# Eight picks of the first search gathered first, head 3's query between the first groups, and another order of slots

## The chip, the cores and the metric

The kernel runs on one core of a Trainium2 chip, in one launch. The metric is the device time of that launch in microseconds (us). Measured before the change: 1631.8 us as the median of 3 runs, from 1630.57 to 1632.56.

The engines are TensorE (PE, matmuls; PEld are its weight loads), VectorE (DVE), ScalarE (ACT), GpSimd (POOL) and SyncE (SP). Each runs its own list of instructions in order, and they wait for each other on semaphores. Data come through 16 DMA engines; transfers are issued by SP, ACT or POOL.

## What is computed

Two transformer blocks over 256 tokens of width 1024, all in float32. The change touches only the end of the second one, a layer that looks up experts (`peer_layer`):

```python
q = (hf @ w_q).reshape(T, PEER_HEADS, 2, PEER_DQ // 2)        # 8 heads, 2 halves of 128
s = jnp.einsum('thpd,hpnd->thpn', q, sub_keys)                # 128 scores for each half
sc, idx = lax.top_k(s, PEER_TOPK)                             # best 16 of each half
cand = (sc[:, :, 0, :, None] + sc[:, :, 1, None, :]).reshape(T, PEER_HEADS, 256)
cidx = (idx[:, :, 0, :, None] * PEER_NKEYS + idx[:, :, 1, None, :]).reshape(T, PEER_HEADS, 256)
top_sc, pos = lax.top_k(cand, PEER_TOPK)                      # best 16 of the 256 sums
eidx = jnp.take_along_axis(cidx, pos, axis=-1)                # 16 of 16384 experts
gate = softmax(top_sc)
act = gelu(einsum('thkd,td->thk', u_tab[eidx], h))
y = einsum('thk,thkd->td', gate * act, v_tab[eidx])
```

So each token and head needs 16 rows of two tables of 16384 x 1024, chosen by the token itself. The result goes through a gain, the residual and a last normalisation to the output.

## The kernel before, in words

**Up to the search.** The dense layers run until about 960 us. Meanwhile SP copies the two expert tables into one table in device memory, `pairs`, whose row holds an expert's u and v (8 KB); a gather of one row for each of 128 tokens is 1 MB. The last dense steps give `rstd` (the norm's factor per token) and `raw` (the residual times its gain). The normed tokens are `u[k] = raw[k] * rstd + shift`, for eight k of 128 features: VectorE does the eight products (L1693, after the first query), ScalarE adds the shift (`shifted`, L1125).

**Queries and scores.** Head 0's query is taken from `raw`, so that it needs no `u`: `first_query(t)` for tile t of 128 tokens scales it on VectorE (L1684) and shifts it on ScalarE (L1114), `first_scores(t)` makes and copies its scores. Heads 1 to 7 are made in halves, `half_head(hd, e)` on TensorE (L2474), copied by ScalarE (L1132), then `all_scores(hd)` (L2440) and `score_copy` (L1137). Before the groups start, TensorE does heads 1, 2 and 3, and four `tok_turn` (L2424), which turn the tokens for the dots; ScalarE copies them (`tok_copy`, L1102). Heads 4 to 7 are put between groups by `HALF_HEADS`: an entry `g: (hd, e)` runs that half right before group g + 1 is weighed.

**The search.** VectorE picks 16 by four steps: `choose_halves` (eight best and their places in each half, L1711 and L1714, and the scores without them, L1719), `choose_rest` (the next eight, and the 256 sums, L1743), `choose_sums` (best 16 of the sums) and `choose_index` (the place in the sums split into two numbers, each looked up by a one-hot product and a sum, L1773 to L1777, and written to `eidx`, L1789). For head 0 the four steps run for tile 0, then for tile 1. For a later head they run for both tiles, one step after each of the first four groups of the head before.

**Rows.** There are 256 rows: row n is pick n % 16 of tile n // 16 % 2 of head n // 32. POOL gathers them in order (L761), each into the slot that `SLOT_AT[n]` names: 11 slots in the arena and 2 in the weight ring (numbers 11 and 12). A gather waits for its indices (`idx_done`), and for its slot: a used one until the row before it there is summed (`row_summed`), and one that holds query weights until that query is made (`q_mm`). Slots 3, 4, 0 and 8 hold the weights of heads 0 to 3, ring slots 11 and 12 those of heads 4 and 5.

```python
SLOT_ORDER = [1, 2, 5, 6, 7, 9, 10] + HEAD_SLOTS          # HEAD_SLOTS = [3, 4, 0, 8]
SLOT_AT = SLOT_ORDER * 3 + [ARENA_SLOTS] + SLOT_ORDER + [ARENA_SLOTS + 1]
```

From row 46 on the 13 slots repeat in that order.

**Groups.** Rows are worked on in groups of four (the last twelve singly). VectorE makes each row's dot with its token (`dot`, L1795); after a group's dots comes a step of the search, if one is due, then the next group's first dot, and then the group's weights (`weights`, L1816: the gelu that ScalarE made, L1166, times the gate). ScalarE makes a diagonal from each weight (L1172), and TensorE multiplies it with the row (`weigh_rows`, L2501), which frees the slot. The gate needs an exponential of ScalarE (`gate_exp`, L1107), for head 0 behind head 2's copies.

Of the kernel before, what the change touches and what calls it, by code (L numbers as in the profile page):

```python
# [23 lines left out]
ALU = mybir.AluOpType  # L24
# [41 lines left out]
HALF_HEADS = {1: (4, 0), 3: (4, 1), 5: (5, 0), 7: (5, 1), 9: (6, 0), 11: (6, 1), 13: (7, 0), 15: (7, 1)}  # L66
FIRST_HEADS = 4
HEAD_SLOTS = [3, 4, 0, 8]
SLOT_ORDER = [1, 2, 5, 6, 7, 9, 10] + HEAD_SLOTS
GAIN_AFTER = 16  # L70
# [113 lines left out]
def program(nc, a, out):  # L184
    ctx = ExitStack()
    with ctx:
# [387 lines left out]
        SLOT_AT = SLOT_ORDER * 3 + [ARENA_SLOTS] + SLOT_ORDER + [ARENA_SLOTS + 1]  # L574
# [26 lines left out]
        def _(sp):  # L601
# [78 lines left out]
            sp.wait_ge(idx_done, score_pieces(HEADS - 1))  # L680
# [10 lines left out]
        def _(pool):  # L691
# [55 lines left out]

            pool.wait_ge(paired, 2 * N_BLOCKS * 16)
            for n in range(ROWS):
                hd, j = divmod(n, HEAD_ROWS)  # L750
                if j == 0:
                    pool.wait_ge(idx_done, score_pieces(hd) if hd else 1)
                elif hd == 0 and j == TOPK:
                    pool.wait_ge(idx_done, TT)
# [11 lines left out]
        def _(act):  # L766
# [376 lines left out]
            for k in range(1, KT):  # L1143
                shifted(k)
            first_query(1)
            first_scores(1)
            for n in range(2 * TT):
                tok_copy(n)
            for hd in range(1, min(HALF_HEADS.values())[0]):
                for e in range(2):  # L1150
                    half_head(hd, e)
                score_copy(hd)
                if hd == 2:
                    gate_exp(0)
# [48 lines left out]
        def _(dve):  # L1203
# [487 lines left out]
            for k in range(KT):  # L1691
                dve.wait_ge(raw_done, k + 2)
                dve.tensor_tensor(u[:, k, 0:SEQ], raw[:, k, 1:1 + SEQ], rstd[:, 0:SEQ], ALU.mult).then_inc(u_scaled, 1)  # L1693
            first_query(1)
# [65 lines left out]
            def choose_index(hd, tiles=both):  # L1760
# [28 lines left out]
                dve.tensor_copy(eidx[:, at:at + len(tiles) * TOPK], part_i[:, 0, ts].rearrange("p t k -> p (t k)")).then_inc(idx_done, 1)  # L1789
# [57 lines left out]
            for t in range(TT):  # L1847
                for part in (choose_halves, choose_rest, choose_sums, choose_index):
                    part(0, [t])
            dve.wait_ge(tok_ev, 4)  # L1850
            parts = (choose_halves, choose_rest, choose_sums, choose_index)
            for g, group in enumerate(GROUPS):
# [17 lines left out]
                if hd < HEADS - 1:  # L1870
                    if at < len(parts):
                        parts[at](hd + 1)
                    if at == len(parts):
                        gate_made(hd + 1)
# [24 lines left out]
        def _(pe):  # L1899
# [615 lines left out]
            first_scores(1)  # L2515
            pe.wait_ge(u_done, 5 * KT)
            for n in range(2 * TT):
                tok_turn(n)
            for hd in range(1, min(HALF_HEADS.values())[0]):
# [113 lines left out]
```

## Time and profile before

The profiled execution took 1637.19 us; its span, from the first to the last instruction, is 1634.8 us, the mean granted TensorE clock 0.968.

| engine | busy us | share of the span | instructions |
|---|---|---|---|
| PE | 1493.5 | 91% | 8220 |
| PEld | 1146.2 | 70% | 8220 |
| DVE | 1080.7 | 66% | 2160 |
| ACT | 554.9 | 34% | 1130 |
| POOL | 563.4 | 34% | 383 |

The transfers of POOL's queue, the gathers, are 268.47 MB and 39.1% of the span of 16 DMA engines. A busy share is a mean over stages of different kinds: PE is busy almost throughout in the dense layers, while from 980 us on the DMA engines are. The page's slices of the span (40 of 40.9 us) show this; the slice that begins near 981 us is the 25th:

```
PE   7999999999999999999999998998987878787877
DVE  7656465765743427998985957666767676758546
DMA  8999968601999997999956939999999999999996
```

Each digit is a busy share in tenths. The chain of waits ends with the gathers too: 17% of the span is their transfers, 13% the weighing.

### The profile page before, as it was taken

The numbers are of one execution on the slowest core, as the hardware profiler recorded it, in microseconds if no ns is written. First come the engines' busy times: TensorE is split into PE (matmuls) and PEld (weight loads), VectorE is DVE, ScalarE is ACT, GpSimd is POOL, SyncE is SP. The second block draws the span as 40 slices with busy tenths as digits, with TensorE's granted clock in tenths as the row PEclk, the third lists the DMA queues.
The fourth block names the chain that finished last, engine by engine and source line by source line (L and its number), as shares of the span: only waits on it lengthen the run. The fifth ranks groups of instructions, "written<-read, shape, count | busy, mean of one in ns | idle before, by whom it ended". The sixth has DMA issues, their size and how long they took to land.

```text
span 1634.8 us, 22787 instructions
## 1 busy us (share of the span) xinstructions
PE 1493.5 (91%) x8220; PEld 1146.2 (70%) x8220; DVE 1080.7 (66%) x2160; ACT 554.9 (34%) x1130; POOL 563.4 (34%) x383
## 2 busy tenths in 40 slices
PE   7999999999999999999999998998987878787877
PEld 7999988777999999998989985544432333333333
DVE  7656465765743427998985957666767676758546
ACT  5434344355444436443116442212121212121213
POOL 3433437210144442001001414554443535454541
PEclk9999999999999999999989999999998989898999
DMA  8999968601999997999956939999999999999996
GB/s 337 370 423 414 418 264 320 213 2 55 360 382 370 372 380 287 372 396 345 361 210 214 378 138 363 426 426 426 427 427 427 427 427 427 427 427 427 427 427 275
DMA packets 99381, 571.90 MB, mean 350 GB/s; under 512 B 11488, under 2 KB 11616, under 8 KB 49632
## 3 DMA queue, kind: packets, MB, share of 16 engines
q1 hardware_dynamic: 60768, 298.15, 47.5%
q0 software_dynamic: 37376, 268.47, 39.1%
q10 hardware_dynamic: 1152, 4.16, 0.7%
q8 instruction: 51, 0.84, 0.2%
q14 instruction: 34, 0.28, 0.1%
HBM read 569.67 MB, written 135.27 MB: 431 GB/s over the span
## 4 chain that ended last, share of the span: by engine, by line
PE 60%; DMA 20%; DVE 14%; ACT 2%; issue 2%; POOL 2%; another core or an unknown queue 0%; SPq 0%; ACTq 0%; DVEq 0%; POOLq 0%
DMA arena<-pairs,eidx 17%; PE ps L2501 13%; PE ps L1916 8%; PE ps L1917 8%; PE ps L1918 8%; DVE arena L1526 3%; PE ps L2005 2%; PE ps L2003 2%; PE ps L2004 2%; PE ps L2474 2%; PE ps L2256 2%; PE ps L2307 1%; POOL w_lo L706 1%; DVE arena L1795 1%; PE ps L1931 1%
## 5 line engine op out<-in xcount | busy, mean ns | idle before, releaser
L2501 PE MATMUL ps<-arena 128*128 128x512 f32 x884 | 420.9, 631 | 84.9 <-ACT arena L1172 84.9
L2501 PEld LDWEIGHTS ps<-arena 128*128 128x128 f32 x884 | 174.7, 202 | 318.6 <-issue 202.6
L1795 DVE CUSTOM_DVE_ANT_0 arena<-arena 128x1024 f32<-128x1024 f32 x221 | 269.2, 1225 | 162.6 <-DMA arena<-pairs,eidx 162.5
L761 POOL DMA_INDIRECT arena<-pairs,eidx x221 | 258.2, 1168 | 311.8 <-PE ps L2501 253.4
L706 POOL TENSOR_TENSOR w_lo<-ring,w_hi 128x1024 fp32r<-128x1024 f32 x81 | 206.1, 2547 | 272.4 <-DVE w_lo L1217 218.1
L1916 PE MATMUL ps<-u_hi,w_hi 128*128 128x256 f32 (+1 forms) x912 | 259.8, 285 | 7.2 <-DVE w_lo L1217 3.9
L1917 PE MATMUL ps<-u_lo,w_hi 128*128 128x256 f32 (+1 forms) x912 | 260.6, 286 | 0.0
L1918 PE MATMUL ps<-u_hi,w_lo 128*128 128x256 f32 (+1 forms) x912 | 259.9, 285 | 0.0
L777 ACT ACTIVATE w_hi<-ring 128x1024 fp32r<-128x1024 f32 x188 | 197.3, 1056 | 147.1 <-PE ps L2005 71.2
L1916 PEld LDWEIGHTS ps<-u_hi,w_hi 128*128 128x128 f32 x912 | 172.9, 190 | 9.2 <-DVE w_lo L1217 4.4
L1918 PEld LDWEIGHTS ps<-u_hi,w_lo 128*128 128x128 f32 x912 | 173.0, 190 | 0.0
L1917 PEld LDWEIGHTS ps<-u_lo,w_hi 128*128 128x128 f32 x912 | 171.9, 189 | 0.0
L1172 ACT ACTIVATE arena<-con,arena 128x128 f32<-128x128 f32 x256 | 82.8, 391 | 208.4 <-DVE arena L1816 207.9
L1217 DVE TENSOR_TENSOR w_lo<-ring,w_hi 128x1024 fp32r<-128x1024 f32 x70 | 93.1, 1330 | 52.0 <-ACT w_hi L777 52.0
L1274 DVE SCALAR_TENSOR_TENSOR arena<-arena,silu_c 128x1536 f32<-128x1536 f32 x32 | 69.9, 2188 | 63.0 <-DMA arena<-in_ada 63.0
L1166 ACT ACTIVATE arena<-arena 128x4 f32<-128x4 f32 (+1 forms) x73 | 15.0, 206 | 262.7 <-DVE arena L1795 262.5
L1526 DVE SCALAR_TENSOR_TENSOR arena<-arena,cols 128x256 f32<-128x256 f32 x240 | 98.4, 481 | 0.0
L2005 PE MATMUL ps<-glu_hi,w_lo 128*128 (+2 forms) x320 | 91.0, 284 | 0.0
L2003 PE MATMUL ps<-glu_hi,w_hi 128*128 (+2 forms) x320 | 90.8, 284 | 0.0
L2004 PE MATMUL ps<-glu_lo,w_hi 128*128 (+2 forms) x320 | 90.8, 284 | 0.0
L706 POOL TENSOR_TENSOR late_lo<-ring,late_hi 128x1024 fp32r<-128x1024 f32 x12 | 29.2, 2432 | 172.0 <-DVE late_lo L1626 150.8
L2501 PE MATMUL ps<-ring,arena 128*128 128x512 f32 x140 | 71.3, 651 | 17.7 <-ACT arena L1172 17.7
(372 smaller groups left out, 2584.6 us busy)
## 6 DMA issues: line engine op xcount, KB each, us to landing
ring<-in_stream SPq DMA_DIRECT2D x126, 1024.0 KB, 7.7
pairs<-in_peer_u SPq DMA_DIRECT2D x128, 512.0 KB, 8.2
pairs<-in_peer_v SPq DMA_DIRECT2D x128, 512.0 KB, 9.2
arena<-in_ada SPq DMA_DIRECT2D x32, 768.0 KB, 9.3
arena<-in_stream SPq DMA_DIRECT2D x4, 1024.0 KB, 9.2
arena<-pairs,eidx POOLq DMA_INDIRECT x221, 16.5
h<-in_x_t SPq DMA_DIRECT2D x1, 1088.0 KB, 5.8
arena<-in_keys ACTq DMA_DIRECT2D x1, 1024.0 KB, 9.1
```

The costliest lines, as they stand in the source:

```text
L706: pool.tensor_tensor(lo[:, half, :], ring[:, slot, e * HALF:(e + 1) * HALF], hi[:, half, :], ALU.subtract).then_inc(used if e else lo_done, 1)
L761: pool.indirect_dma_start(slot_of(n), None, pairs, bass.IndirectOffsetOnAxis(ap=eidx[:, n:n + 1], axis=0)).then_inc(landing(n)[0], 16)
L777: act.activation(w_parts(k)[0][:, half, :], ring[:, slot, e * HALF:(e + 1) * HALF], ACT.Copy).then_inc(hi_done, 1)
L1526: dve.scalar_tensor_tensor(cv[:, m, :], pad_glu[:, m, j:j + SEQ], V("conv_w", j * KT + m), cv[:, m, :], ALU.mult, ALU.add).then_inc(conv_s ...
L1795: dve.tensor_tensor_reduce(row, row, hf[:, n % HEAD_ROWS // TOPK, :], 1.0, 0.0, ALU.mult, ALU.add, dots[:, n % HEAD_ROWS:n % HEAD_ROWS + 1 ...
L1916: pe.matmul(dst, hi[:, half, block], x[0][:, b, 0:w], start=(b == 0), stop=False)
L1917: pe.matmul(dst, hi[:, half, block], x[1][:, b, 0:w], start=False, stop=False)
L1918: mm = pe.matmul(dst, lo[:, half, block], x[0][:, b, 0:w], start=False, stop=(b == KT - 1))
L2003: pe.matmul(ps[:, m, 0:w], w_hi[:, half, block], hi, start=first, stop=False)
L2004: pe.matmul(ps[:, m, 0:w], w_hi[:, half, block], lo, start=False, stop=False)
L2005: mm = pe.matmul(ps[:, m, 0:w], w_lo[:, half, block], hi, start=False, stop=False)
L2501: mm = pe.matmul(ps[:, Y_BANKS[j // TOPK] + half, :], diag[:, n % DIAGS, :], slot_of(n)[:, D + half * 512:D + half * 512 + 512], start=(hd ...
```

## The change

- VectorE's eight products for `u` go to POOL, ahead of its gathers.
- For tile 0 of head 0 a new `first_picks` takes only the eight best of each half, forms their 64 sums and finds the eight best of them, whose experts go to `eidx[:, 0:8]`; then the query of tile 1 is scaled, and `other_picks` finds the remaining eight, by the steps as they were. POOL waits for the first eight indices at row 0, for the next eight at row 8 and for tile 1 at row 16. `idx_done` thereby counts one more.
- TensorE turns the tokens ahead of the scores of tile 1; ScalarE copies in that order. ScalarE makes head 0's exponential behind head 1's copies.
- Head 3 joins the halves between groups, ahead of groups 1 and 2; heads 4 to 7 and the gain are one entry, that is two groups, later. Head 1's search steps are one group later.
- The order of slots: the first ten rows take 1, 2, 5, 6, 7, 9, 10, 3, 4, 0; then twice 1, 2, 5, 6, 7, 9, 10, 3, 8, 4, 0; row 32 takes 11, rows 33 to 43 the same eleven, row 44 again 11, row 45 takes 12.

```diff
@@ -63,11 +63,12 @@
 SINGLE = ROWS - 3 * GROUP
 GROUPS = [slice(n, n + GROUP) for n in range(0, SINGLE, GROUP)] + [slice(n, n + 1) for n in range(SINGLE, ROWS)]
 RING_HEADS = [4, 5]
-HALF_HEADS = {1: (4, 0), 3: (4, 1), 5: (5, 0), 7: (5, 1), 9: (6, 0), 11: (6, 1), 13: (7, 0), 15: (7, 1)}
+HALF_HEADS = {0: (3, 0), 1: (3, 1), 3: (4, 0), 5: (4, 1), 7: (5, 0), 9: (5, 1), 11: (6, 0), 13: (6, 1), 15: (7, 0), 17: (7, 1)}
 FIRST_HEADS = 4
 HEAD_SLOTS = [3, 4, 0, 8]
-SLOT_ORDER = [1, 2, 5, 6, 7, 9, 10] + HEAD_SLOTS
-GAIN_AFTER = 16
+FIRST_SLOTS = [1, 2, 5, 6, 7, 9, 10, 3]
+SLOT_ORDER = FIRST_SLOTS + [8, 4, 0]
+GAIN_AFTER = 18
 FINAL_STEPS = 5
 HALF_D = D // 2
 RESIDUAL_FROM = 44
@@ -571,7 +572,7 @@
 
         Y_BANKS = [0, 2]
         RING_SLOTS = [(BASE["wq"] + hd - FIRST_HEADS) % RING for hd in RING_HEADS]
-        SLOT_AT = SLOT_ORDER * 3 + [ARENA_SLOTS] + SLOT_ORDER + [ARENA_SLOTS + 1]
+        SLOT_AT = FIRST_SLOTS + [4, 0] + SLOT_ORDER * 2 + [ARENA_SLOTS] + SLOT_ORDER + [ARENA_SLOTS] + [ARENA_SLOTS + 1]
         while len(SLOT_AT) < ROWS:
             SLOT_AT.append(SLOT_AT[-SLOTS])
         TURN = [SLOT_AT[:n].count(SLOT_AT[n]) for n in range(ROWS)]
@@ -677,7 +678,7 @@
                 turn = BASE["wq"] + hd - FIRST_HEADS
                 sp.wait_ge(used, turn - (RING - 1))
                 sp.dma_start(ring[:, turn % RING, :], a["stream"][BASE["wq"] + hd]).then_inc(landed[turn % RING], 16)
-            sp.wait_ge(idx_done, score_pieces(HEADS - 1))
+            sp.wait_ge(idx_done, score_pieces(HEADS - 1) + 1)
             sp.dma_start(final_g, a["final_g"].rearrange("(o d) -> o d", o=1).broadcast_to([P, D])).then_inc(final_in, 16)
             sp.wait_ge(fin_step, FINAL_STEPS)
             sp.wait_ge(row_used, ROWS)
@@ -745,13 +746,17 @@
             for piece in range(BASE["w_b"], BASE["wq"]):
                 low(2, piece, piece % RING, 1)
 
+            pool.wait_ge(rstd_done, 5)
+            for k in range(KT):
+                pool.wait_ge(raw_done, k + 2)
+                pool.tensor_tensor(u[:, k, 0:SEQ], raw[:, k, 1:1 + SEQ], rstd[:, 0:SEQ], ALU.mult).then_inc(u_scaled, 1)
             pool.wait_ge(paired, 2 * N_BLOCKS * 16)
             for n in range(ROWS):
                 hd, j = divmod(n, HEAD_ROWS)
                 if j == 0:
-                    pool.wait_ge(idx_done, score_pieces(hd) if hd else 1)
-                elif hd == 0 and j == TOPK:
-                    pool.wait_ge(idx_done, TT)
+                    pool.wait_ge(idx_done, score_pieces(hd) + 1 if hd else 1)
+                elif hd == 0 and j in (TOPK // 2, TOPK):
+                    pool.wait_ge(idx_done, j // TOPK + 2)
                 if TURN[n]:
                     pool.wait_ge(row_summed, held_before(n) + 1)
                 elif SLOT_AT[n] in HEAD_SLOTS:
@@ -1142,15 +1147,15 @@
             first_scores(0)
             for k in range(1, KT):
                 shifted(k)
+            for n in range(2 * TT):
+                tok_copy(n)
             first_query(1)
             first_scores(1)
-            for n in range(2 * TT):
-                tok_copy(n)
             for hd in range(1, min(HALF_HEADS.values())[0]):
                 for e in range(2):
                     half_head(hd, e)
                 score_copy(hd)
-                if hd == 2:
+                if hd == 1:
                     gate_exp(0)
 
             def mean_root(t):
@@ -1688,10 +1693,6 @@
             dve.reciprocal(rstd[:, 0:SEQ], rstd[:, 0:SEQ]).then_inc(rstd_done, 1)
             dve.wait_ge(rstd_done, 5)
             first_query(0)
-            for k in range(KT):
-                dve.wait_ge(raw_done, k + 2)
-                dve.tensor_tensor(u[:, k, 0:SEQ], raw[:, k, 1:1 + SEQ], rstd[:, 0:SEQ], ALU.mult).then_inc(u_scaled, 1)
-            first_query(1)
 
 
             both = range(TT)
@@ -1757,7 +1758,7 @@
                     dve.tensor_tensor(own_gate, own_best, own_best[:, :, 0:1].broadcast_to([P, TT, TOPK]), ALU.subtract
                                       ).then_inc(gate_sub, 1)
 
-            def choose_index(hd, tiles=both):
+            def choose_index(hd, tiles=both, first=0):
 
                 ts = of(tiles)
                 passed()
@@ -1786,7 +1787,52 @@
                 step(dve.scalar_tensor_tensor(part_i[:, 0, ts], part_i[:, 0, ts], float(NKEYS), part_i[:, 1, ts], ALU.mult, ALU.add))
                 passed()
                 at = hd * HEAD_ROWS + tiles[0] * TOPK
-                dve.tensor_copy(eidx[:, at:at + len(tiles) * TOPK], part_i[:, 0, ts].rearrange("p t k -> p (t k)")).then_inc(idx_done, 1)
+                dve.tensor_copy(eidx[:, at + first:at + len(tiles) * TOPK], part_i[:, 0, ts].rearrange("p t k -> p (t k)")[:, first:]
+                                ).then_inc(idx_done, 1)
+
+            def first_picks():
+
+                few = TOPK // 2
+                dve.wait_ge(sc_ev, 1)
+                chains = [(top[:, 0, e], top_u[:, 0, e], own_scores[:, 0, e]) for e in range(2)]
+                eight(chains, 0)
+                sums = cand[:, 0, 0:few * few]
+                step(dve.tensor_tensor(sums.rearrange("p (i j) -> p i j", i=few),
+                                       top[:, 0, 0, 0:few, None].broadcast_to([P, few, few]),
+                                       top[:, 0, 1, None, 0:few].broadcast_to([P, few, few]), ALU.add))
+                passed()
+                step(dve.tensor_copy(top_i[:, 0, :, 0:few], top_u[:, 0, :, 0:few]))
+                eight([(own_best[:, 0], pos_u[:, 0], sums)], 0)
+                passed()
+                step(dve.tensor_scalar(part_u[:, 0, 0, 0:few], pos_u[:, 0, 0:few], 3, None, ALU.logical_shift_right))
+                step(dve.tensor_scalar(part_u[:, 1, 0, 0:few], pos_u[:, 0, 0:few], few - 1, None, ALU.bitwise_and))
+                passed()
+                step(dve.tensor_copy(pos[:, :, 0, 0:few], part_u[:, :, 0, 0:few]))
+                passed()
+                each = [P, 2, few, few]
+                hot = cand[:, 1, 0:2 * few * few].rearrange("p (e i j) -> p e i j", e=2, i=few)
+                iota = C("iota")[:, None, None, 0:few].broadcast_to(each)
+                step(dve.tensor_tensor(hot, pos[:, :, 0, 0:few, None].broadcast_to(each), iota, ALU.is_equal))
+                passed()
+                step(dve.tensor_tensor(hot, hot, top_i[:, 0, :, None, 0:few].broadcast_to(each), ALU.mult))
+                passed()
+                step(dve.reduce_sum(part_i[:, :, 0, 0:few], hot, AX_X))
+                passed()
+                step(dve.scalar_tensor_tensor(part_i[:, 0, 0, 0:few], part_i[:, 0, 0, 0:few], float(NKEYS), part_i[:, 1, 0, 0:few],
+                                              ALU.mult, ALU.add))
+                passed()
+                dve.tensor_copy(eidx[:, 0:few], part_i[:, 0, 0, 0:few]).then_inc(idx_done, 1)
+
+            def other_picks():
+
+                without([(top[:, 0, e], None, own_scores[:, 0, e]) for e in range(2)], [left[:, 0, e] for e in range(2)])
+                choose_rest(0, [0])
+                passed()
+                step(dve.tensor_copy(top_i[:, 0], top_u[:, 0]))
+                without([(own_best[:, 0], None, cand[:, 0])], [left2[:, 0]])
+                passed()
+                eight([(own_best[:, 0], pos_u[:, 0], left2[:, 0])], TOPK // 2)
+                choose_index(0, [0], TOPK // 2)
 
             def dot(n):
 
@@ -1844,9 +1890,11 @@
                 then(dve.scalar_tensor_tensor(acc[:, t, :], acc[:, t, :], fin[:, 8 + t:9 + t], final_g, ALU.mult, ALU.mult),
                      fin_step)
 
-            for t in range(TT):
-                for part in (choose_halves, choose_rest, choose_sums, choose_index):
-                    part(0, [t])
+            first_picks()
+            first_query(1)
+            other_picks()
+            for part in (choose_halves, choose_rest, choose_sums, choose_index):
+                part(0, [1])
             dve.wait_ge(tok_ev, 4)
             parts = (choose_halves, choose_rest, choose_sums, choose_index)
             for g, group in enumerate(GROUPS):
@@ -1868,9 +1916,10 @@
                 if g == 0:
                     gate_made(0)
                 if hd < HEADS - 1:
-                    if at < len(parts):
-                        parts[at](hd + 1)
-                    if at == len(parts):
+                    turn = at if hd else at - 1
+                    if 0 <= turn < len(parts):
+                        parts[turn](hd + 1)
+                    if turn == len(parts):
                         gate_made(hd + 1)
 
             def last_half(half):
@@ -2512,10 +2561,10 @@
             first_scores(0)
             pe.wait_ge(sqrt_done, 5)
             first_query(1, 1)
-            first_scores(1)
             pe.wait_ge(u_done, 5 * KT)
             for n in range(2 * TT):
                 tok_turn(n)
+            first_scores(1)
             for hd in range(1, min(HALF_HEADS.values())[0]):
                 for e in range(2):
                     half_head(hd, e)
```

## Rows read from the trace of the kernel before

**Rows 1.** Windows: us; busy of PE, PEld, DVE, ACT, POOL; PEclk; DMA share; GB/s.

```profile
1010.00:1015.00 5.00, 5.00 (x11) 2.05 (x10) 4.96 (x21) 1.26 (x5) 2.77 (x3) 0.90 0.53 170
...
1072.00:1618.00 546.00, 450.00 (x1030) 200.17 (x1029) 368.47 (x904) 107.80 (x315) 253.22 (x217) 0.93 1.01 426
```

**Rows 2.** Timeline of DVE, dots of six rows: start, us, operation, idle before.

```profile
994.08 1.22 DVE L1795 CUSTOM_DVE_ANT_0 arena<-arena 128x1024 f32<-128x1024 f32 x1 [1.21 <-DMA arena<-pairs,eidx]
...
1016.40 1.23 DVE L1795 CUSTOM_DVE_ANT_0 arena<-arena 128x1024 f32<-128x1024 f32 x1 [0.19 <-DMA arena<-pairs,eidx]
...
1025.18 1.22 DVE L1795 CUSTOM_DVE_ANT_0 arena<-arena 128x1024 f32<-128x1024 f32 x1 [0.91 <-DMA arena<-pairs,eidx]
...
1047.73 1.22 DVE L1795 CUSTOM_DVE_ANT_0 arena<-arena 128x1024 f32<-128x1024 f32 x1 [1.24 <-DMA arena<-pairs,eidx]
...
1072.22 1.23 DVE L1795 CUSTOM_DVE_ANT_0 ring<-ring,arena 128x1024 f32<-128x1024 f32 x1 [1.11 <-DMA ring<-pairs,eidx]
...
1087.88 1.23 DVE L1795 CUSTOM_DVE_ANT_0 arena<-arena 128x1024 f32<-128x1024 f32 x1 [1.22 <-DMA arena<-pairs,eidx]
```

**Rows 3.** Timeline of POOL, issues of rows 0, 11 and 45.

```profile
979.72 1.03 POOL L761 DMA_INDIRECT arena<-pairs,eidx  x1 [29.10 <-DVE eidx L1789]
...
1010.86 0.94 POOL L761 DMA_INDIRECT arena<-pairs,eidx  x1 [6.92 <-PE ps L2501]
...
1087.78 0.94 POOL L761 DMA_INDIRECT ring<-pairs,eidx  x1 [0.31 <-issue]
```

**Rows 4.** Timeline of ACT, copies of scores, bias and tokens.

```profile
967.98 0.39 ACT L1119 ACTIVATE arena<-ps 128x256 f32<-128x256 f32 x1 [0.55 <-PE ps L2440]
...
971.06 0.68 ACT L1114 ACTIVATE arena<-arena 128x128 f32<-128x128 f32 x2
...
974.32 1.09 ACT L1102 ACTIVATE arena<-ps 128x512 f32<-128x512 f32 x2 [0.26 <-PE ps L2424]
...
994.19 0.60 ACT L1137 ACTIVATE arena<-ps 128x512 f32<-128x512 f32 x1 [1.28 <-PE ps L2440]
```

**Rows 5.** Timeline of DVE, steps of tile 0's picks.

```profile
970.11 0.48 DVE L1711 MAX8 arena<-arena 128x8 f32<-128x128 f32 x2
...
971.17 0.07 DVE L1719 MATCH_VALUE_LOAD arena<-arena 128x8 f32 x1
...
975.75 0.18 DVE L1764 TENSOR_SCALAR part_u<-pos_u 128x16 uint32<-128x16 uint32 x1
...
978.64 0.17 DVE L1789 CAST eidx<-arena 128x16 uint32<-128x16 f32 x1
```

**Rows 6.** Groups by line and shape on DVE: busy us, mean ns, idle.

```profile
L1711 DVE MAX8 arena<-arena 128x8 f32<-128x128 f32 x64 | 14.1, 281 | 0.3
...
L1711 DVE MAX8 arena<-arena 128x8 f32<-128x256 f32 x32 | 12.2, 417 | 0.3
```

**Rows 7.** Timeline, a POOL product and a DVE sum beside it.

```profile
933.85 2.38 POOL L706 TENSOR_TENSOR late_lo<-ring,late_hi 128x1024 fp32r<-128x1024 f32 x1 [3.15 <-ACT late_hi L777]
...
934.01 2.51 DVE L1665 TENSOR_TENSOR arena<-arena 128x256 f32<-128x256 f32 x1
```

**Rows 8.** Timeline of PE: turns, head 1, a weighing, a half head.

```profile
972.34 1.04 PE L2424 MATMUL ps<-con,u 128*128 128x128 f32 x8
...
974.61 7.07 PE L2474 MATMUL ps<-u,arena 128*128 128x256 f32 x32
...
1093.38 7.13 PE L2501 MATMUL ps<-arena 128*128 128x512 f32 x16 [1.80 <-ACT arena L1172]
1100.35 3.62 PE L2474 MATMUL ps<-u,ring 128*128 128x256 f32 x16
```

**Rows 9.** Chain of waits: start, us, what.

```profile
986.84 5.67 another core or an unknown queue
...
1004.39 0.60 ACT arena L1137
...
1007.19 10.56 PE ps L2501 x20
```

## Prediction

> **What bounds the kernel now.** I read the slices of the page first: from 980 us on the DMA share is 9 in every slice. The windows say the same: 426 GB/s from 1072 to 1618, one dip at 1010 to 1015 with 53% and 170 GB/s [rows 1]. All of that is the gathers of the second block's last layer, 256 rows of 1 MB. Next the vector engine's dots: where one had to wait for its row, its start is the landing of that row. Rows 3 and 14 start at 994.08 and 1025.18, and row 33, the first that lands in a ring slot, at 1072.22 [rows 2]. From row 14 to 33 that is 2.48 us a row, and 2.45 over its last ten rows (row 23 at 1047.73); I use 2.45. From row 3 to 14 eleven rows should take 26.95 us and take 31.1: the dip costs 4.15. So the last 650 us are: time of the first issue, plus 256 rows at a fixed pace, plus holes in the queue. Nothing that the engines save between holes counts.
>
> The first issue comes at 979.72 on POOL, and waits there 29.1 us for the first indices [rows 3]. The hole is the issue of row 11 at 1010.86, the first that needs a used slot: eleven rows were under way, and row 0 was summed only then. Its dot starts at 1016.40, 5.5 us after an issue into a dry queue [rows 2, 3].
>
> **Earlier start.** The first eight picks now need one eight-fold maximum per half, 64 sums, one maximum and a short index. Scores of tile 0 are copied by 968.37 [rows 4]; the vector engine began only at 970.11, behind its eight products and the second query, which both leave this place. Step by step [rows 5]: two maxima and two finds 970.11 to 971.17, 1.06. A maximum of 128 elements is 281 ns, of 256 it is 417 [rows 6], so 1.06 ns an element; by that slope an estimate for 64 sums is 0.24 with its start, for the maximum over them 0.25, for its find with load 0.33, and 0.10 for a cast. The index part took 975.75 to 978.81, 3.06; its three passes shrink from 512 to 128 elements, 0.41 each: 1.84. Sum 3.82, from 968.45 to 972.3. From the end of the cast at 978.81 to the issue was 0.91, so the first issue could be at 973.2, 6.5 earlier.
>
> The eight products move to POOL. One of 128x1024 took 2.38 there [rows 7], so 0.6 to 0.8 for 256 columns as an estimate: from 964.5 (rstd ready) to about 970.5, still before the picks end; behind them on POOL stand only the gathers. Beside that POOL product a vector sum of two SBUF operands of 256 elements, where a maximum of 256 takes 0.42 [rows 6], took 2.51: it ended 0.3 after POOL's [rows 7]. first_picks has such instructions (the sums at 969.5, later the one-hot). The least wait is 0, one POOL product is 0.8, the end of the series at 970.6 is 1.1; at the far end POOL also loses 0.3 between products, all are over at 973 and the sums wait until then: 3.5. I take 0.4, since the wait in the row ended with the one product beside it: first issue 973.6, **-6.1** (-6.5 to -5.4, far end -3).
>
> The Trainium skill (SBUF — State Buffer, "two separate sides") says that a vector instruction with two SBUF inputs and a GpSimd instruction exclude each other for the whole instruction. The 2.51 row agrees; were the sums held to the end of all eight products, the start would be worth about 3, which is rival C below.
>
> **Ten rows instead of eleven before a used slot.** Rows 0 to 7 take free slots (slot 3 after head 0's query), row 8 slot 4 after head 1, row 9 slot 0 after head 2; row 10 waits for row 0's sum. Head 3 leaves the front, so only heads 1 and 2 (13.9 us of products) stand ahead. They begin later: tokens are turned before the second scores. Turns start at about 971.4, once the last product is shifted, not 972.34; from there to the end of the last copy it was 3.07 [rows 4, 8], then the bias (0.68) and the scores (an estimate of 0.6, being four products of 128 columns): 975.8 against 974.61, +1.1. The copy of head 2's scores, before at 994.19 to 994.79, so ends at 995.9; without the stretch of 5.67 in which the chain saw no known releaser, 2.2 more than the 3.5 of products in it, at 993.7. From the end of head 3's copy (1004.99) to the first weighing (1007.19) was 2.2 [rows 9]; the gate's exponent is ready by then, since ACT now does it behind head 1 and tile 1's picks end near 988.5. So the first weighing starts at 995.9 to 998.1, I take 997.0. The vector side isn't later: tile 1's picks follow at 979.8 or so and take what tile 0's took, 8.7 [rows 5], to 988.5; five dots of 1.23 [rows 2] and half a us for the gate bring 995.2. From 1007.19 to the issue of row 11 was 3.7: row 10 is issued at 1000.7 and lands 5.5 later, 1006.2. Without a hole it would land 31.5 us after the first issue, 1005.1. **Hole +1.1** (0 to 2.2), in place of the old **-4.15**.
>
> **Head 3 and 4 between the groups.** TensorE now has no slack until row 32: five weighings after the idle took 10.56 [rows 9], four take 6.97 later, a half head 3.5, half of the 7.07 of head 1 [rows 8]. Rows 0 to 3 end at 1005.8, head 3's first half 1009.3, row 4 at 1011.0. Row 14 takes its slot, lands at 1016.6, and would at 1016.0: **+0.6** (0 to 1.5). Rows 4 to 7 end at 1016.3, the second half 1019.8; row 18 (slot 8) lands in time by 0.9. Then 8 to 11, an estimate of 0.9 for scores, 12 to 15, half of head 4, 16 to 19, 20 to 23, the other half: 1055.7. Row 32 goes to a ring slot and needs that: it lands at 1061.4 and is due at 1060.7. The 6.97 holds a start out of idle, so less: **+0.4** (0 to 1.5). Head 1's picks, one group later, are ready (index about 1035).
>
> **Row 45.** Here is what I think decides. Row 45 takes slot 12, head 5's weights, now used up at group 10, behind the weighing of rows 36 to 39; before, two groups earlier, and its issue at 1087.78 [rows 3] met a full queue. Rows 40 to 44 alone cover it. From row 39's landing to the weighing of rows 36 to 39 was 5.5 (1087.88 to 1093.38: choose_rest, dot, weights), the weighing 6.97, the half head 3.5 [rows 2, 8], POOL 0.2, landing 5.5: 21.7. Due is 6 rows, 14.7. **Hole +7.0**: the least is 6.4, and 8.4 if landing takes the 7.0 of row 0 (row 3's landing less three rows, after 979.72).
>
> Costed at nothing: head 5 to 7 and gain later (their scores are needed a head later; TensorE was idle 1.80 ahead of 1093.38 already [rows 8], and from row 46 on there are thirteen slots as before); counts of idx_done; the query of tile 1 and the last eight picks (index near 980.3, while rows 0 to 7 are issued at 1.25 until 983).
>
> Sum: -6.1 - 4.15 + 1.1 + 0.6 + 0.4 + 7.0 = **-1.15**. The span of 1634.8 becomes 1633.65; the profiled execution, 1637.19 with 2.4 around the span, 1636.0. It lies 5.4 above the median 1631.8; by the same step the median becomes **1630.6**.
>
> **Rivals.**
> A. No hole at row 45: the queue is deeper than I count, or the half head comes before the weighing. For: before, the queue was deep there, row 45 being due 14.8 after its issue. Against: row 44 is issued near 1076 and lands at 1090.3, four us before row 45's issue. Without the 7.0: -8.15, 1623.6.
> B. Slower: TensorE stalls once more as in the 5.67 piece, with all gathers in the queue, between rows 36 and 45, where each us lengthens the hole. Price 2.2 to 5.7: 1632.8 to 1636.3. From 1.2 of stall on it is slower than before. For: before it happened once just after the queue had filled. Against: none of that length in the chain after 1007.
> C. The early start is lost, sums behind all eight products: -3 instead of -6.1, so 1633.7. For: the 2.51 row. Against: no row shows a wait over more than one product.
>
> **Numbers.** The forecast gets 0.63, with its own range -6.5 - 4.15 + 6.4 = -4.3 to -5.4 - 4.15 + 2.2 + 0.8 + 0.5 + 8.4 = +2.4, so 1627.5 to 1634.2. A 0.14, B 0.13, C 0.10. 0.2% is 3.3 us, about what a measurement tells from none. Faster by that (below 1628.5): A and 0.15 of the forecast, 0.29. Slower (above 1635.1): half of B, 0.07, 0.02 of C, 0.04 of the forecast, 0.13. Within: 0.58. The range of 8 in 10 leaves out A and a part of B: 1625 to 1635.
>
> **What would show it.** First issue at 973 to 974.5; the dip at 1010 gone or a us long; a new dip in DMA near 1089 to 1096, POOL's issue of row 45 waiting for a half head's product (line of half_head on PE) for some 17 us behind row 44's. Wrong if that issue waits less than 10 us, if DMA has no dip there, or if a stall sits between rows 0 and 45 that is none of the three.

## The result: 0.2% slower, and the profile after

The changed kernel takes 1636.3 us (median of 20 runs, 1631.82 to 1639.55), the kernel before in the same series 1632.49 (20 runs): a ratio of 1.0021, 95% interval 1.0013 to 1.0028. The medians lie 3.8 us apart; the interval reads 2.1 to 4.6 us. The forecast was 1630.6, in a range up to 1635, worked out from a median of 1631.8 before. The profiled execution took 1635.37.

Page of the changed kernel: span, busy time by engine, two of the lines of 40 slices (of 40.8 us).

```profile
span 1632.5 us, 22798 instructions
...
PE 1491.7 (91%) x8220; PEld 1142.9 (70%) x8220; DVE 1079.9 (66%) x2162; ACT 554.4 (34%) x1130; POOL 570.8 (35%) x391
...
DMA  8999968502999997999955949989999999999996
GB/s 338 377 423 423 422 258 345 177 2 72 373 369 367 375 381 289 370 393 346 364 203 209 408 187 404 393 341 427 427 427 426 427 426 428 427 428 427 427 427 281
```

The 27th slice, a 9 before, is an 8 now, with 341 GB/s, and the 26th has 393. The windows of the changed kernel (columns as in [rows 1]) find the places:

```profile
1010.00:1015.00 5.00, 5.00 (x18) 3.09 (x17) 1.44 (x3) 0.39 (x1) 2.82 (x3) 1.00 0.99 392
1050.00:1060.00 10.00, 9.25 (x31) 5.05 (x30) 4.59 (x9) 0.59 (x2) 6.21 (x6) 1.00 0.75 291
1089.00:1096.00 7.00, 5.73 (x22) 3.91 (x21) 4.75 (x19) 1.54 (x5) 2.17 (x2) 1.00 0.13 20
1072.00:1618.00 546.00, 448.42 (x1020) 199.51 (x1020) 362.53 (x880) 108.26 (x316) 249.05 (x212) 0.92 0.99 419
```

The dip of 1010 to 1015 (53% in [rows 1]) is gone: this profile lies 4.4 us earlier, as shown below, but from 1005.6 to 1010.6 it has 93% too. A small dip stands at 1050 and the forecast one at 1089, with 13% and 20 GB/s. Now POOL's timeline (start, us, what, idle before and its releaser): the eight products, then the issues of rows 0, 32, 44 and 45.

```profile
960.11 5.17 POOL L752 TENSOR_TENSOR u<-arena,rstd 128x256 f32<-128x256 f32 x8 [13.89 <-DVE rstd L1693]
968.81 1.03 POOL L766 DMA_INDIRECT arena<-pairs,eidx  x1 [3.53 <-DVE eidx L1824]
...
1052.27 1.92 POOL L766 DMA_INDIRECT ring<-pairs,eidx  x1 [7.87 <-PE ps L2523]
...
1076.80 0.93 POOL L766 DMA_INDIRECT ring<-pairs,eidx  x1 [7.51 <-PE ps L2550]
1093.35 1.24 POOL L766 DMA_INDIRECT ring<-pairs,eidx  x1 [15.61 <-PE ps L2523]
```

Rows 32 and 45 are released by a half head's product (line 2523), row 45 16.6 us behind row 44. VectorE's timeline: rstd's end, the sums of the first picks, the dots of rows 30 to 33, 43, 45 to 47.

```profile
958.28 1.75 DVE L1693 RECIPROCAL rstd<-rstd 128x256 f32<-128x256 f32 x1 [2.14 <-ACT rstd L1102]
...
965.05 0.30 DVE L1800 TENSOR_TENSOR arena<-arena 128x64 f32<-128x64 f32 x1
...
1052.15 1.23 DVE L1841 CUSTOM_DVE_ANT_0 arena<-arena 128x1024 f32<-128x1024 f32 x1 [1.22 <-DMA arena<-pairs,eidx]
1054.59 1.23 DVE L1841 CUSTOM_DVE_ANT_0 arena<-arena 128x1024 f32<-128x1024 f32 x1 [1.21 <-DMA arena<-pairs,eidx]
1058.81 1.23 DVE L1841 CUSTOM_DVE_ANT_0 ring<-ring,arena 128x1024 f32<-128x1024 f32 x1 [2.99 <-DMA ring<-pairs,eidx]
...
1062.22 1.23 DVE L1841 CUSTOM_DVE_ANT_0 arena<-arena 128x1024 f32<-128x1024 f32 x1 [2.11 <-DMA arena<-pairs,eidx]
...
1087.13 1.23 DVE L1841 CUSTOM_DVE_ANT_0 arena<-arena 128x1024 f32<-128x1024 f32 x1 [1.19 <-DMA arena<-pairs,eidx]
...
1099.20 1.23 DVE L1841 CUSTOM_DVE_ANT_0 ring<-ring,arena 128x1024 f32<-128x1024 f32 x1 [5.34 <-DMA ring<-pairs,eidx]
1102.32 1.23 DVE L1841 CUSTOM_DVE_ANT_0 arena<-arena 128x1024 f32<-128x1024 f32 x1 [1.88 <-DMA arena<-pairs,eidx]
1104.74 1.22 DVE L1841 CUSTOM_DVE_ANT_0 arena<-arena 128x1024 f32<-128x1024 f32 x1 [1.19 <-DMA arena<-pairs,eidx]
```

The reciprocal of rstd ends at 958.6 to 964.4 us in three profiles of the kernel before and at 960.0 to 966.6 in three of the changed one, so from here on times are counted **from that end** (964.44 before, 960.03 here). The "landing" of a row is the start of its dot where that had to wait for it, and a "hole" is time that the queue of gathers loses against its pace of 2.45 us a row. Row 47 lands at 143.0 before and at 144.7 after, though the first issue went from 15.3 to 8.8. Behind row 47 all profiles take the same, 527.3 to 529.5.

### The profile page after: what moved, and what is told of

It is laid out like the page before. It is cut to its first block, busy times and chain, and to the rows that moved or that the text cites. A ratio compares the mean times of both kernels' runs of the same rounds, so it can differ in the third digit from the quotient of the medians.

```text
span 1632.5 us, 22798 instructions
## 1 busy us (share of the span) xinstructions
PE 1491.7 (91%) x8220; PEld 1142.9 (70%) x8220; DVE 1079.9 (66%) x2162; ACT 554.4 (34%) x1130; POOL 570.8 (35%) x391
## 4 chain that ended last, share of the span: by engine, by line
PE 61%; DMA 19%; DVE 13%; ACT 3%; issue 2%; POOL 2%; SPq 0%; ACTq 0%; DVEq 0%; POOLq 0%
DMA arena<-pairs,eidx 16%; PE ps L2550 14%; PE ps L1965 8%; PE ps L1967 8%; PE ps L1966 8%; DVE arena L1531 3%; PE ps L2523 2%; PE ps L2054 2%; PE ps L2052 2%; PE ps L2053 2%; PE ps L2305 2%; PE ps L2356 1%; DVE arena L1841 1%; POOL w_lo L707 1%; DMA ring<-pairs,eidx 1%
## 5 line engine op out<-in xcount | busy, mean ns | idle before, releaser
L1222 DVE TENSOR_TENSOR w_lo<-ring,w_hi 128x1024 fp32r<-128x1024 f32 x70 | 87.8, 1255 | 62.7 <-ACT w_hi L782 62.7
L1279 DVE SCALAR_TENSOR_TENSOR arena<-arena,silu_c 128x1536 f32<-128x1536 f32 x32 | 75.6, 2370 | 50.4 <-DMA arena<-in_ada 50.4
L2550 PE MATMUL ps<-ring,arena 128*128 128x512 f32 x140 | 76.6, 691 | 29.4 <-ACT arena L1177 29.4
## 6 DMA issues: line engine op xcount, KB each, us to landing
arena<-pairs,eidx POOLq DMA_INDIRECT x221, 16.6
```

Of the source, the lines that this page charges most:

```text
L2550: mm = pe.matmul(ps[:, Y_BANKS[j // TOPK] + half, :], diag[:, n % DIAGS, :], slot_of(n)[:, D + half * 512:D + half * 512 + 512], start=(hd ...
```

## The experiments

**Slots 11 and 12 used later.** Theory H: the added time is two waits for a ring slot that still holds head 4's or head 5's weights. The first edit is of row 45 alone, the second of both rows.

```diff
-SLOT_AT = FIRST_SLOTS + [4, 0] + SLOT_ORDER * 2 + [ARENA_SLOTS] + SLOT_ORDER + [ARENA_SLOTS] + [ARENA_SLOTS + 1]
+# slot 12 first at row 50
+SLOT_AT = ... + [ARENA_SLOTS] + SLOT_ORDER[:5] + [ARENA_SLOTS + 1]
+# slot 11 first at row 36, slot 12 at row 52
+SLOT_AT = (FIRST_SLOTS + [4, 0] + SLOT_ORDER * 2 + SLOT_ORDER[:4] + [ARENA_SLOTS] + SLOT_ORDER[4:] + SLOT_ORDER[:4]
+           + [ARENA_SLOTS] + SLOT_ORDER[4:7] + [ARENA_SLOTS + 1])
```

> The changed kernel with one difference: ring slot 12 (head 5's weights) is first used by row 50 instead of row 45; rows 45 to 49 take arena slots again. Theory H (the loss is holes in the gather queue where a row waits for a ring slot): the hole at row 45, 7.2 us at that row and 0.7 behind it in the trace of the changed kernel, goes; 7 to 8 us faster than the changed kernel (1636.3), so 1628 to 1629.5, which is 3 to 4.5 below the kernel before. Rival S (the loss sits in the new first stage: POOL's products beside VectorE, tokens turned before scores, head 3 between groups): no change, within 2 us of the changed kernel.

> The changed kernel with both ring slots used later: slot 11 first by row 36 instead of 32, slot 12 first by row 52 instead of 45. Theory H: the hole at row 32 (2.7 us in the trace) goes too, so 10 to 10.5 us below the changed kernel, 1625.5 to 1626.5, and no dip of DMA after row 14. Rival S: within 2 us of the changed kernel.

Measured: 1627.75 (0.9978 of the kernel before, 0.9967 to 0.9989) and 1627.52 (0.9964, 0.9951 to 0.9977). No hole at row 45 in either; row 47 lands at 136.0 and 135.9 instead of 144.7. Row 45's wait is shown. Row 32's, added to it, can't be told from none by these times, though the second edit was expected to gain another 2.5 us or so.

**The half heads early instead, and slot 12 two rows later.**

```diff
+HALF_HEADS = {0: (3, 0), 1: (3, 1), 2: (4, 0), 3: (4, 1), 5: (5, 0), 7: (5, 1), 9: (6, 0), 11: (6, 1), 13: (7, 0), 15: (7, 1)}
+GAIN_AFTER = 16
# the second kernel, with the changed halves:
+SLOT_AT = ... + [ARENA_SLOTS] + SLOT_ORDER[:2] + [ARENA_SLOTS + 1]
```

> The changed kernel with its slots as they are, and only the half heads put back to where the kernel before had them: both halves of head 4 by group 3, of head 5 by groups 5 and 7 (head 3's halves stay behind groups 0 and 1). So slots 11 and 12 are free two groups sooner, though rows 32 and 45 still use them. Theory H (both holes are waits for a ring slot that its head's weights still hold): issues of rows 32 and 45 meet a full queue, the 2.8 us and 7.8 us at rows 32 and 45 are gone, and TensorE, with four half heads in a row, may leave up to 3 us between rows 18 and 30: row 47 lands 134 to 137 us after rstd (144.7 in the changed kernel), 1626 to 1629.5. Rival L (the order of slots itself, with one of thirteen slots fewer in use before row 45, makes the queue dry whatever the half heads do): a hole of 5 us or more stays at row 45, 1633 to 1636. Rival T (TensorE is the bound once the halves are early): holes of 3 to 7 us between rows 18 and 30, 1630 to 1634.

> The changed kernel with the first use of slot 12 moved by two rows, from row 45 to row 47; rows 45 and 46 take used slots of rows 33 and 34. Theory H: the slot comes free at the same time, about 133.3 us after rstd, and two more rows cover the wait, so the hole of 7.2 us at row 45 becomes one of 7.2 - 2 x 2.45 = 2.3 us at row 47 (1.5 to 3.2), with about half a us behind it; 1636 - 5 = 1631 (1629.5 to 1632.5). Rival (the length of the hole is that of a restart of a dry queue, whatever covers it): 6 us or more at row 47, 1635 to 1637. Rival (no hole at 47, some other row's wait was taken): none, 1627.5 to 1629.

Measured: 1628.11 (0.9968, 0.9957 to 0.9980), row 47 at 136.0; and 1631.0 (0.9983, 0.9972 to 0.9994), row 47 at 139.8. POOL's timeline with the halves early, rows 44 and 45: no wait between them, so rival L falls. Rival T falls too: rows 16 to 31 lose 0.9 us, where it has 3 to 7.

```profile
1079.33 0.94 POOL L766 DMA_INDIRECT ring<-pairs,eidx  x1 [5.37 <-PE ps L2550]
1080.57 1.93 POOL L766 DMA_INDIRECT ring<-pairs,eidx  x1 [0.30 <-issue]
```

With slot 12 at row 47 its issue still waits for the half head, 1095.92 less 961.75 being 134.2, but two more rows cover it:

```profile
1095.92 1.03 POOL L766 DMA_INDIRECT ring<-pairs,eidx  x1 [10.62 <-PE ps L2523]
```

From row 43 (127.75) to row 47 (139.79) are 12.04 us for four rows, a hole of 2.2, where 2.3 was worked out. So both uses of the slot agree with one rule: a hole is the time from the last landing until the slot is ready and its own row has landed, less 2.45 for each row that lands in between.

**The parts alone.** The early start with the halves, slots and gain of the kernel before; and the reverse, the old search with the changed halves and slots, first bare, then with the two moves that belong to them.

```diff
# e4 to e7: the moves
-                if hd == 2:
+                if hd == 1:
                     gate_exp(0)
...
-                    if at < len(parts):
-                        parts[at](hd + 1)
+                    turn = at if hd else at - 1
+                    if 0 <= turn < len(parts):
+                        parts[turn](hd + 1)
...
```

> The changed kernel with the halves of heads, the order of slots and the place of the gain as before the change: eight first picks, POOL's products, the new order of turns and scores are alone. Theory H: gathers start 6.5 us earlier, but row 11 still waits for row 0's sum behind heads 1 to 3, which isn't earlier; its hole grows by what the start gains: 1631 to 1633.5, no change against before (1632.5), with a dip of some 8 to 10 us near row 11 and none at rows 32 and 45. Were the start worth its 6.5 by itself: 1626. Rival S: about the 1636 of the changed kernel.

> The kernel before with only the halves of heads, the order of slots and the place of the gain of the changed kernel; the first search and the products as before. Theory H: no hole at row 10, 14 or 32, since rows are due 6.5 us later there, the old hole of 4.6 at rows 11 to 14 gone, the hole at row 45 of 7.2 to 7.9 as in the changed kernel: 2.5 to 3.5 above before, 1635 to 1636. Rival S: head 3 in the loop aside, nothing of the first stage is new, so no loss: 1632.5 or less.

> The run with the kernel before's search and the changed halves and slots (1644.0), and in addition the two moves that belong to the halves: the gate's exponent behind head 1 on ScalarE instead of head 2, and the search steps of head 1 one group later on VectorE. Theory H (1644 came of the gate and of head 1's first step standing ahead of the first weighing): the first weighing starts 33 to 35.5 us after rstd instead of 39.0, no hole at row 10 or one below 1.5, about 0 to 1.5 at row 32, 7 to 8 at rows 45 and 46: row 47 at 145 to 149 us after rstd (153.0 without the moves), 1635 to 1638. Rival (the late search itself, 6.5 us later, delays all of TensorE's weighings): stays at 151 or more, 1641 to 1645.

Measured: the start alone 1629.51 (0.9986, 0.9977 to 0.9995), which is 0.8 to 3.8 us faster than before by the interval, where no change was expected. Its one profile doesn't show the gain, as row 47 lands at 142.1, inside what the kernel before has (139.8 to 143.0). Row 11 is issued at 46.0, as before (46.4), since it waits for row 0's weighing: most of the 6.5 us becomes a longer hole. The reverse without the moves 1643.96 (1.0069, 1.0054 to 1.0083), a miss of theory H by 8 us. Its trace (ACT, DVE, PE; columns as above) shows why:

```profile
992.99 0.23 ACT L1108 ACTIVATE arena<-arena 128x32 f32<-128x32 f32 x1
...
993.25 0.18 DVE L1802 TENSOR_REDUCE arena<-arena 128x2 f32<-128x32 f32 x1 [1.09 <-ACT arena L1108]
...
993.78 0.42 DVE L1733 COPY arena<-arena 128x512 f32<-128x512 f32 x1
...
997.23 1.21 DVE L1796 CUSTOM_DVE_ANT_0 arena<-arena 128x1024 f32<-128x1024 f32 x1
...
998.37 0.16 DVE L1817 TENSOR_TENSOR arena<-arena 128x4 f32<-128x4 f32 x1
...
999.02 8.66 PE L2502 MATMUL ps<-arena 128*128 128x512 f32 x16 [7.98 <-ACT arena L1173]
```

The gate's sum waits for the exponential behind head 2, then head 1's first search step (993.78 to 997.23) stands ahead of the fifth dot, and the first group's weights (998.37) come only behind that dot, so TensorE stood 7.98 us before the first weighing. With both moves the weighing starts at 33.9 instead of 37.7 (the 39.0 of the expectation was misread) and the time is 1639.31 (1.0042, 1.0027 to 1.0057), row 47 at 148.6: the landing is as expected, the time 1 us above. The two moves are worth 4.4 us at row 47, and the prediction carries them without a price; halves and slots without the early start cost 6.9 us (4.4 to 9.3).

**The eight products back on VectorE** (with slots 11 and 12 later).

```diff
-            pool.wait_ge(rstd_done, 5)
-            for k in range(KT): pool.tensor_tensor(u[:, k, 0:SEQ], ...)
+            for k in range(KT): dve.tensor_tensor(u[:, k, 0:SEQ], ...)   # behind first_query(0), ahead of first_picks()
```

> The run with slots 11 and 12 used later (1627.5), with the eight products of the query's input put back from POOL onto VectorE, ahead of the first picks. The first issue comes 1 to 2 us later. Theory H (the start before row 10 is partly lost to the wait of row 10 for its slot): the landings from row 14 on are 0 to 1 us later than in that run, 1627 to 1629. Rival 1 (each us of the start is a us of the end): 1 to 2 us later from row 14 to the end, 1628.5 to 1629.5. Rival 2 (POOL's products held VectorE up all the same): the first issue is not later, or even sooner, 1626.5 to 1627.5. The time alone can't tell these apart, the first issue and the landings can.

Measured: 1627.05 (0.9963, 0.9949 to 0.9978), the same as with the products on POOL. The first issue is at 9.2 instead of 8.8, no more: VectorE makes the eight in 2.77 us, mostly in time in which it waits for the scores anyway. The early start is owed to the shorter search with the second query behind it, and hardly to POOL.

```profile
963.64 2.77 DVE L1695 TENSOR_TENSOR u<-arena,rstd 128x256 f32<-128x256 f32 x8
...
967.38 0.20 DVE L1800 TENSOR_TENSOR arena<-arena 128x64 f32<-128x64 f32 x1
```

**TensorE's clock ahead of the first weighing.** In the runs so far the first four weighings took 7.1 us in the changed kernel's profile and 8.6 to 10.1 in the others with its search and halves. Two kernels fill TensorE's idle 2.84 us ahead of them (slots 11 and 12 later in both): with head 3's first half, or with that product as an unused double.

```diff
+HALF_HEADS = {-1: (3, 0), 0: (3, 1), 3: (4, 0), 5: (4, 1), 7: (5, 0), 9: (5, 1), 11: (6, 0), 13: (6, 1), 15: (7, 0), 17: (7, 1)}
# the other kernel, with the changed halves:
+            half_head(3, 0, counted=False)
             for g in range(len(GROUPS)):
```

> The run with slots 11 and 12 used later (1627.5), with head 3's first half put ahead of the first weighing and its second half behind group 0 (keys -1 and 0 instead of 0 and 1). In five of six profiles with this search TensorE idled 2.84 us ahead of the first weighing, the granted clock fell to 0.50 and the four weighings took 8.6 to 10.1 us; in the profile of the changed kernel the clock stayed at 1.00 and they took 7.1. Theory K (the holes at rows 10 to 14, 3 to 4.7 us in most runs, come from this low clock and from the half heads between the groups): the half head fills the idle stretch, the clock stays at 1.00, the first weighing starts at 31.8 after rstd and takes 7.1, row 10 is issued at 34.1 instead of 35.2, row 14 lands at 50.5 to 52 instead of 54.5, no hole at row 23: row 47 lands 132.5 to 134.5 after rstd (135.9), 1624 to 1626.5. Rival: the idle stretch isn't the cause of the low clock, weighing from 31.8 at 0.50, row 14 not earlier than 53.5 and 1627 to 1628.5.

> The run with slots 11 and 12 used later (1627.5), with the product of head 3's first half computed once more, unused, in the idle stretch of TensorE ahead of the first weighing; the real halves stay where they are. Only the clock can gain. Theory K: granted clock 1.00 at the first weighing, which starts 0.65 later (31.8 after rstd) and takes 7.1 us instead of 10.1, row 10 issued at 34.1 instead of 35.2, row 14 lands 1 to 2 us sooner than 54.5: 1626 to 1627. Rival (the clock falls whatever TensorE does there): the weighing takes 9.7 to 10.1 from 31.8 on, all is 0.6 later, 1628.

Measured: 1624.75 (0.9955, 0.9941 to 0.9969) and 1624.93 (0.9947, 0.9933 to 0.9962). PE's timeline without the filling, and a window at its start (columns: us, PE busy, PEclk, DMA share, GB/s):

```profile
992.74 10.10 PE L2551 MATMUL ps<-arena 128*128 128x512 f32 x16 [2.84 <-ACT arena L1178]
```

```profile
992.74:995.59 2.85, 2.85 (x4) 0.50 1.03 437
```

The same two views with the double, ahead of the weighing and in it:

```profile
990.45 3.62 PE L2524 MATMUL ps<-u,arena 128*128 128x256 f32 x16
993.91 7.03 PE L2552 MATMUL ps<-arena 128*128 128x512 f32 x16
```

```profile
990.30:993.45 3.15, 3.15 (x17) 1.00 1.00 421
993.45:997.45 4.00, 4.00 (x12) 1.00 1.01 428
```

0.50 is the lower of the clock's two levels, 1.2 GHz. With TensorE busy ahead of the weighing it is granted 2.4 GHz in the one profile of each kernel, and row 10 is issued at 33.8 instead of 35.2. That the filling is the cause is likely but not shown: the changed kernel's first profile had 2.4 GHz behind the same 2.84 us of idle time. Nor is a gain in time shown. Both ratios are 0.1 to 0.2% below that of the run they build on, but the intervals overlap; row 47 lands at 134.6 and 135.1 instead of 135.9, and at 134.9 in the run with the products on VectorE, which fills nothing (the first of the two has a hole of 1.6 us around row 27 whose cause stays open). Both beat the kernel before, by 7.3 (5.1 to 9.6) and 8.7 us (6.2 to 10.9).

**Both kernels again.**

> The changed kernel once more, nothing altered. Its profiled execution landed row 47 only 1.7 us later after rstd than the kernel before, where the median of its runs is 3.8 us later. Theory K: that execution was the rare one in which the first weighing ran at full clock; most run it at 0.50 as five of the six others with this search did, row 10's issue at 35.2 instead of 33.4 and row 14's landing 53 to 54.5 instead of 52.25; then row 47 lands at 145.5 to 147.5 after rstd, holes at rows 32 (2.5) and 45 (7.8) as they were, 1635.5 to 1637. Rival (the rest stands elsewhere, in the dense stage or at the end): row 47 again at 144.7 and the time 1636.

> The kernel before once more, nothing altered. Two profiles of the changed kernel land row 47 at 144.7 and 144.0 us after rstd, the one profile of the kernel before at 143.0: 1.0 to 1.7 of the 3.8 us that the medians differ by. Theory M: the one profile of before was late between rstd and row 47 as well as ahead of rstd (its granted clock was 0.69 to 0.74 in the products of head 2 and 0.65 at the first weighing); in most executions row 47 lands at 140 to 142 after rstd. Rival D: row 47 lands at 143 again and the rest stands ahead of rstd, which then ends 2 us sooner (959 to 960) in the kernel before than in the changed kernels (961 to 962 in most). Rival E: it stands behind row 47 (527.3 to 528.7 us to the end in all so far).

> The kernel before a third time, for how much one execution differs from the next: theory M row 47 at 140 to 142 after rstd, rival D 143 with rstd's end at 959 to 960.

> The changed kernel a third time: by both theories row 47 at 144 to 146.5 after rstd, a hole of 6 to 8 us at rows 45 and 46 and of 1 to 3 at rows 32 and 33; by rival D rstd ends at 961 to 962.

Measured: the changed kernel 1636.33 again (1.0023, 1.0014 to 1.0032). Row 47 lands at 144.7, 144.0 and 144.9 in three profiles of it, at 143.0, 139.8 and 142.8 in three of before. So theory M holds in part: one execution of three of the kernel before was 3 us earlier, and its window at the first weighing (columns as in the last windows) had the full clock:

```profile
1001.33:1005.33 4.00, 4.00 (x11) 1.00 0.86 315
```

while the third profile of before had, at the same place,

```profile
1003.45:1007.45 4.00, 3.94 (x5) 0.57 0.60 254
```

and row 11's issue 3 us later (46.5 against 43.4). About half of this stands ahead of the weighing, which begins at 41.2 and at 42.8: head 3's products take 7.07 and 8.72 us.

```profile
988.27 7.07 PE L2474 MATMUL ps<-u,arena 128*128 128x256 f32 x32
```

```profile
990.32 8.72 PE L2474 MATMUL ps<-u,arena 128*128 128x256 f32 x32
```

Over these the granted clock was 1.00 in the first 4 us of the one, 0.58 of the other. What theory K says of the changed kernel falls: its second and third profile, with 0.50 at the first weighing, land row 47 at 144.0 and 144.9, no later than the first at the full clock. On the means the traces hold 2.7 of the 3.8 us up to row 47, which lies inside the interval. Where the rest stands isn't settled: rstd ends 1.6 us later in the changed kernel on the mean of three, but within either kernel it differs by some 6, and rival D is neither borne out nor refuted by that. Rival E falls, the time behind row 47 being the same in all.

## Why the prediction was wrong

Lateness of a row is its landing less (first issue + 14.3 + 2.45 a row behind row 3), from [rows 2, 3]; the rows below show how much of it is gained in each stretch. Means of three profiles each, us:

| | predicted | before | after | measured |
|---|---|---|---|---|
| first issue | -6.1 | 15.3 | 8.8 | -6.5 |
| lateness gained up to row 15 | -4.15 + 1.1 + 0.6 = -2.45 | 3.4 | 2.5 | -0.9 |
| rows 16 to 31 | 0 | 0.4 | 0.8 | +0.4 |
| rows 32, 33 | +0.4 | 0 | 1.7 | +1.7 |
| rows 34 to 43 | 0 | 0.7 | 0.9 | +0.2 |
| rows 44 to 47 | +7.0 | 0 | 7.7 | +7.7 |
| sum | -1.15 | | | +2.7 |

- **Earlier start**: right. The first issue comes 8.8 us after rstd, which on the scale of the trace before is 973.2, the prediction's figure without any wait. The products took 0.65 each (5.17 for eight), inside the estimate. Rival C's loss did not come, but what it rests on was hardly put to the test: the products ended at 965.28, only 0.23 behind the start of the sums at 965.05. The Trainium skill (SBUF — State Buffer, "two separate sides") would have the sums wait for the product under way. The trace leaves this open: they took 0.30, against 0.20 in the run with the products on VectorE.
- **Row 45**: the mechanism is as put, and its rule held when the row was moved (2.2 for 2.3). From row 39's landing to row 45's issue were 16.4 us in all three profiles, where the prediction adds up 16.2, and row 45 landed 5.85 later for 5.5. The stretch measured 7.7 for 7.0: the rows behind a restart are late too (row 46 by 0.7 to 1.3), and the prediction gave the restart no aftermath. Rival A is refuted. Rival B's stall did not come on top of the 16.4, TensorE's longest idle time between 1070 and 1093 us being 2.44; that its far end, 1636.3, is the measured time is chance.
- **The step that failed is the sizing of the small holes**: "lands 5.5 later", from row 11 alone, with nothing behind it. Row 32's issue came at 91.9 to 92.2 (the prediction's 1055.7 is 91.3), but it landed 5.8 to 6.6 after it, and row 33 was late by another 0.3 to 1.0: +1.7 where +0.4 stood. Likewise rows 11 to 15 behind row 10: 0.5 to 2.4, on the mean 1.6, where 0.6 stood. Together +2.3. No run shows why a landing takes longer at one restart than at another.
- **The old hole** was read from one execution, 4.15; over three it is 1.8 to 4.2, mean 3.35: +0.8. The granted clock ahead of and at the first weighing differs between these executions. The 10.56 for five weighings in [rows 9] was at the lower clock (0.57 in its first 4 us) and was noted as coming after the idle, not as something that an execution may or may not have.
- **Row 10** came out right in size (0.9 for 1.1) partly by luck: it is issued at 33.4 to 35.2, where the prediction's 1000.7 is 36.3, and lands 5.5 to 7.3 behind its issue instead of 5.5.
- **The range**: its upper end counts 0.8 and 0.5 for the two holes whose own ranges go to 1.5. With these the forecast's own range would have reached +4.05, that is 1635.9.

Nearly all of this leans one way (only the start and row 10 were 0.4 and 0.2 better), and the gain of -1.15 was smaller than the error at rows 32 and 33 alone: the sign rested on terms that one row of one execution could not carry. Of the 5.7 us between the forecast and the measured time, 0.7 is the time before, 1632.49 over 20 runs where the forecast started from 1631.8.

## What to carry to other kernels

When transfers set the end, an earlier start is worth only what the next wait for a buffer leaves of it: here 6.5 us at the start left 0.8 to 3.8 by themselves, and 3.6 and 5.9 once slots that come free late were given to rows with enough issues ahead of them. List, for every slot, when it comes free and how many rows cover the wait; a restart of a dry queue cost its latency here and 0.7 to 1.3 us more at the row behind row 45. Read such small terms from several executions, and look at the clock of each.

## What the hardware showed that was not expected

An issue on POOL that starts beside a dot on VectorE ends about 0.81 us after the dot does. Row 32's took 1.92 us where most take 0.94, and ended at 1054.19, 0.81 after the dot that began at 1052.15 and ended at 1053.38. In the kernel before two issues of this kind (1023.16 and 1038.07) end 0.82 after their dots too. In the changed kernel's trace 120 of the 256 issues start while a dot runs. Of these 99 take over 1 us, and each of the 99 ends 0.80 to 0.83 after its dot; nearly all the others start in the dot's last 0.2 us. Of the 136 issues that start beside no dot 7 take over 1 us.

The Trainium skill (SBUF — State Buffer, "two separate sides") says that a GpSimd queue's descriptors are held up while VectorE runs an instruction in a two-port mode, and names a copy of fp32; an instruction with two SBUF inputs it counts among those that take the shared ports, against a GpSimd instruction that reads SBUF. Here the hold-up stands beside dots of two fp32 inputs.

It isn't what lengthened row 32's landing: in the changed kernel's third profile that issue started beside no dot and took 0.94, and the row landed 6.6 us after it all the same.

```profile
1058.55 0.94 POOL L766 DMA_INDIRECT ring<-pairs,eidx  x1 [7.22 <-PE ps L2523]
...
1065.13 1.23 DVE L1841 CUSTOM_DVE_ANT_0 ring<-ring,arena 128x1024 f32<-128x1024 f32 x1 [2.28 <-DMA ring<-pairs,eidx]
```
